# TensorE products without a reader, placed ahead of the routers, the counts, the first gathers and the norms

## What is computed

```python
def first_block(...):
    ...
    x = x + mod_x[:, 2] * merge_branches(y_gdn, y_sgu, x_gates, w_a, w_b, w_o)
    hx = modulate(rms_norm(x, norm_ffn_g), mod_x[:, 3], mod_x[:, 4])
    x = x + mod_x[:, 5] * hier_moe(hx, ...)  # top-1 of 4 groups, then top-2 of 8 experts; 32 experts, 256 wide
    return rms_norm(x, final_norm_g)

def second_block(x, ...):
    h = token_mixer(x, ...)                 # stick-breaking and dilated attention, 16 heads
    x = layer_norm_2(ALPHA * x + h, ln1_g, ln1_b)
    h = grouped_moe(x, ...)                 # 16 experts, 1024 wide, group of 4, top-2
    return layer_norm_2(ALPHA * x + h, ln2_g, ln2_b)
```

## Time and profile before

| | us |
|---|---|
| median of 3 runs | 1799.36 |
| lowest, highest | 1798.74, 1804.3 |
| the profiled execution, its own time | 1801.51 |
| its span in the trace | 1799.8 |
| TensorE busy in the span | 1623.7 (90%) |
| mean granted clock of TensorE | 0.959 |

### The profile page before, as it was taken

The page is one execution under the profiler, slowest core; times in us unless marked ns, Lnnn a source line. Parts: engine busy times, 40 slices in busy tenths (PEclk is TensorE's granted clock), DMA queues, the critical chain, the costliest instruction groups (busy, mean ns, idle before and its releaser), DMA issues.

```text
span 1799.8 us, 21591 instructions
## 1 busy us (share of the span) xinstructions
PE 1623.7 (90%) x8392; PEld 1049.0 (58%) x8392; DVE 549.5 (31%) x1122; ACT 329.6 (18%) x664; POOL 174.0 (10%) x180
## 2 busy tenths in 40 slices
PE   5799999999999989979998789998889998999886
PEld 1466666776588868865554369757534543443333
DVE  2266666667520011153122110382500111001002
ACT  2223333433331100021011011341200000000001
POOL 1244343344300000000000000000000000000000
PEclk8799999999999988979999899999899999999998
DMA  9311110111734423419999974103399999999993
GB/s 392 149 54 41 41 47 23 47 35 47 304 139 154 147 87 105 173 50 366 421 421 421 421 287 151 60 1 122 143 417 421 377 368 421 421 362 385 421 421 140
DMA packets 59645, 404.92 MB, mean 225 GB/s; under 512 B 6782, under 2 KB 7938, under 8 KB 13232
## 3 DMA queue, kind: packets, MB, share of 16 engines
q1 hardware_dynamic: 53328, 381.92, 53.3%
q0 software_dynamic: 6240, 21.92, 4.2%
HBM read 402.71 MB, written 1.10 MB: 224 GB/s over the span
## 4 chain that ended last, share of the span: by engine, by line
PE 70%; DMA 17%; DVE 8%; issue 2%; ACT 1%; SPq 1%; DVEq 0%; POOL 0%; POOLq 0%; ACTq 0%
PE bank L602 69%; DMA ring<-in_moe 15%; DVE arena L1631 2%; DMA ring<-in_dense 2%; ACT arena L1264 1%; DVE arena L1662 1%; DVE arena L1678 1%; PE bank L1020 1%; DVE arena L1667 0%; DVE arena L1659 0%; DVE arena L1657 0%; DVE arena L1671 0%; DMA arena<-decay_rows 0%; DVE arena L1681 0%; SPq L434 0%
## 5 line engine op out<-in xcount | busy, mean ns | idle before, releaser
L602 PE MATMUL bank<-ring,arena 128*64 128x512 f32 (+2 forms) x2304 | 519.3, 602 | 60.3 <-DMA ring<-in_moe 58.6
L602 PEld LDWEIGHTS bank<-arena 128*128 128x128 f32 (+2 forms) x2864 | 375.9, 192 | 125.2 <-ACT arena L1264 47.8
L602 PE MATMUL bank<-arena 128*128 128x128 f32 (+3 forms) x2864 | 422.9, 298 | 27.2 <-DVE arena L1681 6.8
L602 PEld LDWEIGHTS bank<-ring,arena 128*64 128x64 f32 (+2 forms) x2304 | 173.8, 137 | 370.2 <-issue 365.0
L1264 ACT ACTIVATE arena<-bank 128x256 f32<-128x256 f32 (+1 forms) x369 | 164.3, 452 | 1175.4 <-PE bank L602 879.2
L602 PE MATMUL bank<-hc,head_w 128*128 128x512 f32 (+1 forms) x384 | 164.8, 536 | 3.1 <-DMA head_w<-in_head_w 3.1
L1997 DVE TENSOR_TENSOR arena<-arena,bank 128x256 f32<-128x256 f32 x48 | 20.2, 421 | 360.2 <-ACT arena L1264 360.2
L602 PE MATMUL bank<-arena,ring 128*128 128x256 f32 x512 | 116.3, 387 | 4.3 <-ACT arena L1264 2.6
L602 PEld LDWEIGHTS bank<-arena,ring 128*128 128x128 f32 x512 | 99.2, 194 | 19.8 <-ACT arena L1264 3.4
L602 PE MATMUL bank<-hc,ring 128*128 128x256 f32 x512 | 110.7, 379 | 0.0
L602 PEld LDWEIGHTS bank<-hc,ring 128*128 128x128 f32 x512 | 97.2, 190 | 13.2
(11 more groups left out here) (245 smaller groups left out, 1054.2 us busy)
## 6 DMA issues: line engine op xcount, KB each, us to landing
ring<-in_moe SPq DMA_DIRECT2D x288, 1024.0 KB, 13.1
ring<-in_dense SPq DMA_DIRECT2D x72, 1024.0 KB, 7.1
head_w<-in_head_w POOLq DMA_DIRECT2D x27, 512.0 KB, 4.0
arena<-decay_rows POOLq DMA_DIRECT2D x16, 256.0 KB, 4.6
xc<-in_xc SPq DMA_DIRECT2D x1, 2048.0 KB, 8.2
arena<-bias_rows POOLq DMA_DIRECT2D x2, 1024.0 KB, 8.7
mats<-in_square SPq DMA_DIRECT2D x1, 1088.0 KB, 11.2
out_y<-xc SPq DMA_DIRECT2D x2, 512.0 KB, 2.9
```

Of the source, the lines that this page charges most:

```text
L602: return nc.tensor.matmul(out, lhsT, rhs_, start=start, stop=stop, **kw)
```

## The change

A helper `keep_warm(n)` issues n products of 128x128 ones with 512 columns of constant matrices (`mats`: the unit matrix, two triangles and a block mask) into bank 7. Nothing reads them, they wait for no semaphore and raise none. 18 of them are placed: for each mixture two ahead of the router's products, two ahead of the counts and two ahead of the first gather (12); one before and one after the norm's sums behind the first mixture (2); two ahead of the output projection of the second block (2); one ahead of each `variance_sum` (2).

```diff
--- before.py
+++ after.py
@@ -645,6 +645,11 @@
                         if k == 0:
                             release(ins)
                 return ins
+
+            def keep_warm(n):
+
+                for _ in range(n):
+                    mm(bank[7][:, :], ones[:, :], mats[:, 0:4, :].rearrange("p a b -> p (a b)"))
 
             def column_sum(out, src, n=KT):
 
@@ -940,6 +945,7 @@
             def route(m, width, experts):
 
 
+                keep_warm(2)
                 pe.wait_ge(s["router_landed"], 16 * (m + 1))
                 src = H if m == 0 else X
                 logits = [bank[5][:, qt * width:(qt + 1) * width] for qt in range(QT)]
@@ -1125,8 +1133,10 @@
 
             route(0, GROUPS1 + E1, E1)
             mixture(0)
+            keep_warm(1)
             for k in range(KT):
                 norm_sum(1, k)
+            keep_warm(1)
 
             n2 = 0
             for j in range(O20):
```

## The result

| | median us | lowest, highest | runs |
|---|---|---|---|
| before | 1799.19 | 1798.74, 1804.3 | 4 |
| the change | 1788.18 | 1786.17, 1788.58 | 4 |

The ratios of this document are those on record; they are not the quotient of the two medians, from which they differ by up to 0.0009, or 1.6 us. The profiled execution of the change took 1788.58 us with a span of 1786.9, against 1801.51 and 1799.8 before. TensorE's mean granted clock went from 0.959 to 0.972, and its busy time rose from 1623.7 to 1625.3 us although 18 products (36 records) came in.

The account below looks back on a forecast made before the run. Mixtures were bound by TensorE and the weight stream running level, router stretches by a TensorE-VectorE chain partly at half clock. 4.8 + 3.4 + 4.9 = 13.1 us from 1801.5 gives 1788.4, forecast 1788.5, range 1784 to 1797.0.

Parts of the forecast that it names:

- Router one: Stretch around the first mixture's router: products, counts and first gather at fuller clock, together 4.8 us gained.
- Products: Router's products behind unread pairs: router one 2.5 us, 24 records at full clock and 8 at half; router two 0.4 us.
- Counts: Count records behind a pair: 0.8 us in router one, limited by VectorE's own routing part; net 1.0 us in router two.
- Gather to `up`: First gather at full clock, about 3.8 instead of 5.81 us; 1.5 us gained in router one, cut by VectorE's ranking.
- Router two: Stretch around the second mixture's router: products 0.4, counts 1.0 and gather 2.0 us, together 3.4 us gained.
- Norms and projection: Sums behind mixture one 1.7, last variance sums 1.7, output projection 1.5 us: together 4.9 us gained at full clock.
- Nothing late next: Mixtures: an earlier gather starts the weight stream and ends the mixture earlier by the same amount; nothing else becomes late.
- The rule of the Trainium skill on transposes: Rival: transposes do not engage full clock, so both routers' counts stay at half clock; 1790.5 us, chance 0.06.
- The narrow products undo it: Rival: clock falls late under the routers' products, both routers gain at most 1 us, norms and projection keep 4.9; 1795.6, chance 0.14.
- Own time or median: Whole kernel: gains taken from the profiled 1801.5 us; its 2.15 us above the median read as removable clock drops, not subtracted again.

Follow-up runs that it names:

- the norms' kernel: The change with only the six products at the norms and ahead of the output projection, without the twelve around the routers; 1795.72 us, ratio 0.9969 to before.

## Why the prediction was right

The mechanism is as predicted: the same instructions run at full clock behind the unread products. That the sum came out within 0.2 us of the measured difference (13.1 and 12.9) is luck. The total of each router moves by about 2 us from one execution to the next, and three stretches that were forecast to stay moved by up to 1.4 us.

- **Router one**, forecast 4.8 us, measured 4.48. Products: the stretch from the last norm sum to the end of the products fell from 9.82 to 7.63 us, 2.2 (forecast 2.5); the clock lasted 2.7 us of them, as assumed. Counts: from `kept` to the gather 5.73 became 4.98, 0.75 (0.8). Gather to `up`: 6.67 became 5.13, 1.54 (1.5), with VectorE's ranking as the cap, as said: TensorE waits 1.32 us there now instead of 0.85. The size is in part luck: in the second profiled execution of the same kernel the first gather took 5.44 us, and this router took 25.00 us, a gain of 3.45.
- **Router two**, forecast 3.4, measured 4.01. Products 1.0 instead of 0.4: the clock fell later than in the execution before. In other kernels with the same pair, or transposes in its place, these products took from 3.75 to 5.77 us, so this term is chance. Counts 1.02 (1.0); gather 1.99 (2.0). Both routers together gain 8.49 us in this trace and 5.3 to 9.5 us in the five other traces that have all twelve products or transposes around them; the forecast of 8.2 lies within.
- **Norms and projection**, forecast 4.9, measured 1.69 + 1.55 + 1.66 = 4.9. These repeat: every trace with unread wide products or transposes there has them within 0.1 us, and both traces with none lose them.
- **Nothing late next**: right. The mixture's stream starts 4.58 us sooner, and mixture one kept its length (+0.41). Mixture two was 1.4 us longer, attention 1.22 shorter; neither was forecast, and they nearly cancel. The same stretches differ as much between other profiled executions (mixture two 501.3 to 503.6, attention 152.2 to 155.0).
- **The rule of the Trainium skill on transposes** was given 0.06 and is refuted by the kernel with transposes. Its price was not taken from the forecast's own terms: the counts of router two stand there with 1.0 us and here with 1.2, so it should read 1790.3 and not 1790.5.
- **The narrow products undo it**, given 0.14: half true. In the traces with the pairs the clock fell under them or under the transposes behind them; only with four products ahead of the first router did it not. But it came back under the transposes or the pair, so counts and gathers gained.
- **Own time or median**: the step was right, its reason wrong. I took the sum from the profiled execution's 1801.5 and explained its distance to the median by clock drops that it had and others had not. All 34 runs of the kernel before have a median of 1802.4 and a mean of 1801.9. The profiled one was ordinary, and the first runs shown were low. Against the 30 later runs the change is worth 14 us, near the sum of 13.1, and not the 10.9 that I set against 1799.36. My expectation of 2.5 to 5 us for the norms' kernel rested on the belief that a typical execution loses less there than the profiled one; both traces without products at the norms lose the same 4.9 us. The 6.55 us of that kernel are more than its places can give in any trace here. The rest may be scatter, or drops of the clock elsewhere: attention, where nothing was placed, took 154.7 and 154.9 us in the two traces without products at the norms and 152.2 to 153.5 in eleven of the twelve others (155.0 in one). That is not shown to come from the change.

## What to carry to other kernels

Where TensorE stands for two or more microseconds ahead of work that is on the path, look at the granted clock of that work: at half clock it took up to nearly twice its time here (7.04 us against 3.76), and unread wide products that fit into the pause can win that back at no cost. Size them to the pause at full clock, put them behind the last instruction that someone waits for, and use wide products or transposes; narrow ones failed in the routers and at the projection. Look at more than one execution: the first gather kept the clock in half of the traces with a pair ahead of it. Where the work behind the pause is itself narrow, shorten it first: the clock falls under it, and filling alone gives only its first few microseconds.

## What the runs showed of the hardware

- TensorE busy without a gap is not enough in the routers. Fillers of 16 columns took the same 1.85 us and left the first router's products at 7.04 us; fillers of 512 columns and transposes of 128 columns brought them to 4.72 and 4.75. In all, the narrow fillers changed the time by a ratio of 0.9998, the others by 14 us. Ahead of the norms' sums 0.96 us of narrow fillers went with full clock (3.72 us).
- In the gating, where records with one row of ones alternate with full ones, each record of 128 columns takes 0.21 us at full clock and 0.36 at half. With the full ones four in a row it is 0.16 (0.65 us from 665.79 to 666.44) and 0.29; transposes take 0.11 at full clock (sixteen in 1.8 us). That the alternation is what costs fits these numbers, but was not tried by itself.
- The time of one kernel scatters: 1798.7 to 1805.9 before, 1786.2 to 1790.6 for the change over eight runs. Part of it arises ahead of anything changed, and goes with the clock there. Up to the gating eleven traced kernels have the same instructions, and its products start between 660.31 and 664.76 us. In the norms' kernel they start 3 us sooner than in the kernel before, and from 20 to 60 us its clock is 0.91 and 0.83 (two windows of 20 us) against 0.79 and 0.76.
